# Recurrent block: the lower levels' products in four groups of 32 stationary columns, and a new order of a level's steps on VectorE

## The chip, the cores and the metric

One core of one Trainium2 chip runs the whole program. The metric is the device time of one execution in microseconds (us). The engines are named as in the profile: PE (TensorE's matmuls), PEld (its weight loads), DVE (VectorE), ACT (ScalarE), POOL (GpSimd), SP (SyncE, which here only issues DMAs).

## The reference

The program computes two transformer-like blocks in a row over 256 tokens with 1024 features, in fp32. The change touches only the HGRN2 mixer, the first mixer of the second block. It has 8 heads of 128 key features and 128 value features:

```
proj = h @ w_in                      # (256, 4096), split in q, fz, inp, og
q = silu(q);  f = lb + (1 - lb) * sigmoid(fz);  k = 1 - f;  logf = log(f)
# per head, with a state S of 128 x 128:
#   S_t = diag(f_t) S_{t-1} + (1 - f_t) inp_t^T ;   o_t = S_t^T q_t
cum    = cumsum(logf)
scores[t, s] = sum_n q[t,n] * k[s,n] * exp(cum[t,n] - cum[s,n])     for s <= t
o[t]   = sum_s scores[t, s] * inp[s]
y      = (rms_norm(o, out_norm) * sigmoid(og)) @ w_out
```

## The kernel before

**The streamed weights.** All weights come as 374 parts of 128x1024 fp32 through a ring of four buffers (`raw`). ACT rounds a part to a high half (`hi`, L315), DVE subtracts it from the part to get the low half (`lo`, L779), and PE multiplies high by high, high by low and low by high (L1541 to L1543, for token tiles L1663 to L1665). PE waits for `lo_ready` ahead of a tile; `multiplied` is a wait for `part_done`, by which PE tells that it has used a part. A call `step(name, j)` on DVE is `lo` for the part three behind part j of that phase. A tile goes to one of four PSUM banks (0 to 3), and PE may not begin tile n before tile n-4 is evicted (`free_bank`, on the semaphore `evacuated`).

**The recurrence as levels.** The 256 tokens are two halves of 128 (index z), the second in reversed order. In a half, the scores between tokens are made by levels. Level 0 is the diagonal, level 1 neighbours, and level l (2 to 7) takes blocks of 2^l tokens: keys of the early half of a block against queries of its later half, both decayed to the block's middle, so that no exponent is positive. Level 8 is between the two halves. One level needs, in this order:

- `level_args(l)` on DVE: two subtractions of 128x1024 (`args_later`, L1168, and `args_earlier`, L1172) write the exponents of queries and keys into the buffer `EB[l % 2]`. It waits on `lev_mm` until the matmuls of level l-2, which read the same buffer, are done. For level 8 it is one subtraction (L1179).
- `level_decay(l)` on ACT: exp over the buffer, 128x2048 (L624).
- `level_queries(l)` on DVE: the queries times their decay, 128x1024 (L1190), which raises `x_up`.
- `level_mm(l)` on PE (L1845): for each head one fp32 matmul with 128 stationary columns (all keys of the head) and 128 moving ones (64 queries of either half). `pair_mm` (L1832) makes levels 0 and 1 with 64 moving columns, one matmul for a head and half. Results go to banks 4 to 7, two banks for a level (g = 0, 1), `lev_mm` counts the banks. An fp32 matmul leaves two records in the trace.
- `take(l)` for levels 0 to 5 on DVE (L1205): two predicated copies of 128x512 from PSUM into the score matrix `PD`, under the mask `LM` (which pairs belong to the level). `take_wide(l)` for levels 6 and 7 on ACT (L638) copies rectangles. `lev_sel` counts both.

**The order around it.** The mixer's stage `hi` (the input part, 8 parts in four pairs, `hi_tile(n, tok)` for a pair n and a half) and `hg` (the gate, `hg_tile(t)`, 8 parts) run on PE between the levels: `hi_tile(0,0)`, `pair_mm(0)`, `hi_tile(0,1)`, `pair_mm(1)`, and then for l = 2 to 7 two tiles and `level_mm(l)`: `hi_tile(2,·)`, `hi_tile(4,·)`, `hi_tile(6,·)`, `hg_tile(0)` and `(1)`, `(2)` and `(3)`, `(4)` and `(5)`. Then `hg_tile(6)`, `across_mm` (level 8, L1855), `hg_tile(7)`, and the eight heads' outputs (`head`, L1893 to L1895), mixed with the first tiles of the output projection `ho`. PE, DVE and ACT each have their order written out by hand; SP loads a part as soon as its buffer is free. A `hi_tile(n,0)` needs the low halves of parts n and n+1, `hg_tile(t)` that of part t; `hg` follows `hi` in the stream, so part hg+t is part hi+8+t. On DVE the loop before is

```
for l in range(3, LEVELS + 1):
    level_args(l)
    if l - 2 < TAKEN: take(l - 2)
    n = 2 * (l - 2)
    step("hi", n)
    level_queries(l)
    if l >= 7: gate_evict(2 * (l - 7)), gate_evict(2 * (l - 7) + 1)
    step("hi", n + 1)
```

`gate_evict(t)` (L810) empties the bank of `hg_tile(t)`. ACT makes the high halves in `token_pair` and `gate_tile`, between its `level_decay`s.

Of the kernel before, what the change touches and what calls it, by code (L numbers as in the profile page):

```python
# [15 lines left out]
I32 = mybir.dt.int32  # L16
# [4 lines left out]
P = 128  # L21
S = 256
D = 1024
C = D // P
# [44 lines left out]
LEVELS, TAKEN = 8, 6  # L69

# [3 lines left out]
def build(nc, stream, par_d, x_d, wf_d, table_d, onehot_d, ident_d, mask_d, lmask_d, out_d):  # L74
    scr = nc.dram_tensor("bias_rows", [H_MOBA, P, EXT], F32, kind="Internal")
    row = nc.dram_tensor("bias_row", [H_MOBA, EXT], F32, kind="Internal")
    with ExitStack() as ctx:
# [57 lines left out]
        LM = flat(F[:, 48:51, :]).bitcast(I32).rearrange("p (l z j) -> p l z j", l=TAKEN, z=2)  # L135
# [11 lines left out]
        U_CUM, U_KK, U_CK, U_QS, U_PD, U_EB = 8, 16, 16, 24, 68, (0, 60)  # L147
# [23 lines left out]

        H_REV, RSTD_REV = u_two[:, 2 * C:3 * C, :, 0:P], F[:, 51, 0:P]
# [133 lines left out]
        def _(act):  # L306
# [319 lines left out]
            def take_wide(l):  # L626
# [3 lines left out]
                for g in range(2):  # L630
                    act.wait_ge(lev_sel, 2 * l + g)
                    act.wait_ge(lev_mm, 2 * l + g + 1)
# [6 lines left out]
                    last.then_inc(lev_sel, 1)  # L639

# [9 lines left out]
            for t in range(0, 4, 2):  # L650
                gate_tile(t)
                gate_tile(t + 1)
                level_decay(7 + t // 2)
            take_wide(6)
# [6 lines left out]
            for g in range(2):  # L661
                act.wait_ge(lev_mm, 2 * LEVELS + g + 1)
                A(PX[:, 4 * g:4 * g + 4, :], bank[4 + g][:, :].rearrange("p (h t) -> p h t", h=4),
                  ACT.Copy).then_inc(px_copied, 1)
# [104 lines left out]
        def _(dve):  # L769
# [405 lines left out]
            def level_args(l):  # L1175

                dve.wait_ge(lev_mm, 2 * (l - 1))
# [14 lines left out]
            def take(l):  # L1192
# [3 lines left out]
                n = P // b  # L1196
                for g in range(2):
                    if l >= 1:
                        dve.wait_ge(lev_sel, 2 * (l - 1) + g + 1)
                    dve.wait_ge(lev_mm, 2 * l + g + 1)  # L1200
                    half = early(U_PD, 1) if l == 0 else later(U_PD, l)
                    dst = half[:, :, 4 * g * n:4 * (g + 1) * n, :].rearrange("p z (c n) i -> p z c n i", c=4)
                    pick = LM[:, l:l + 1, :, :].rearrange("p l z (n i) -> p z l n i", i=h)
                    src = bank[4 + 2 * (l % 2) + g][:, :].rearrange("p (z c n i) -> p z c n i", z=2, c=4, i=h)
                    v.copy_predicated(dst, pick.to_broadcast([P, 2, 4, n, h]), src).then_inc(lev_sel, 1)  # L1205
# [11 lines left out]
            dve.wait_ge(pd_zero, 1)  # L1217
# [5 lines left out]
            level_queries(2)  # L1223
            step("hi", 1)
            for l in range(3, LEVELS + 1):
                level_args(l)
                if l - 2 < TAKEN:
                    take(l - 2)
                n = 2 * (l - 2)
                step("hi", n)  # L1230
                level_queries(l)
# [137 lines left out]
        def _(pool):  # L1369
# [70 lines left out]
            g.memset(PD, 0.0).then_inc(pd_zero, 1)  # L1440
            for pair in range(2):
# [83 lines left out]
        def _(pe):  # L1525
# [299 lines left out]
            def pair_mm(l):  # L1825

                keys, queries = (KK_T, early(U_QS, 1)) if l == 0 else (EB_T[1], later(U_QS, 1))
                for g in range(2):
                    for c in range(4 * g, 4 * g + 4):
                        for z in range(2):  # L1830
                            o = z * S + c % 4 * (P // 2)
                            last = mm(bank[4 + 2 * l + g][:, o:o + P // 2], keys[:, z, c, :],  # L1832
                                      queries[:, z, c * (P // 2):(c + 1) * (P // 2), 0], start=True, stop=True)
                    last.then_inc(lev_mm, 1)

            def level_mm(l):
# [3 lines left out]
                pe.wait_ge(x_up, l - 1)  # L1840
                for g in range(2):
                    pe.wait_ge(lev_sel, 2 * (l - 2) + g + 1)
                    out = bank[4 + 2 * (l % 2) + g][:, :].rearrange("p (z c j) -> p z c j", z=2, c=4)
                    for c in range(4 * g, 4 * g + 4):
                        last = mm(out[:, :, c % 4, :], keys[:, c, :], queries[:, :, c, :], start=True, stop=True)  # L1845
                    last.then_inc(lev_mm, 1)

            def across_mm():

                pe.wait_ge(x_up, LEVELS - 1)  # L1850
                for g in range(2):
                    pe.wait_ge(lev_sel, 2 * (LEVELS - 2) + g + 1)
# [48 lines left out]
            pe.wait_ge(lev_sel, 2 * LEVELS)  # L1901
# [176 lines left out]
```

## Time and profile before

| | us |
|---|---|
| median of three runs (1168.82 to 1169.49) | 1168.86 |
| the profiled execution, whole | 1168.89 |
| its span, first to last instruction | 1167.1 |
| PE busy in the span | 1149.9 |
| DVE busy | 877.7 |
| ACT busy | 697.2 |
| POOL busy | 380.7 |

The profile is of one execution. A group of rows below is either of the page (busy time and share of the span for each engine), of a timeline (start and length in us, engine, line of the kernel, output and inputs, and in brackets the idle time of the engine before it and what released it), of the waits (who waited for whom, us in total, times, longest), or of groups of instructions by line and shape (count, busy us, mean ns of one). "128*64 128x128" is a matmul over 128 rows with 64 stationary and 128 moving columns. Ends of matmuls are modelled, and two matmuls in a row overlap in their lengths, so a pace is read from start to start.

### The profile page before, as it was taken

The page shows a single profiled execution, that of the slowest core. Times are in us where ns is not written, and L with a number is a line of the kernel's source. Part 1 is how long each engine was busy: PE and PEld are TensorE (multiplying, and loading weights), DVE is VectorE, ACT ScalarE, POOL GpSimd, SP SyncE. Part 2 cuts the span into 40 slices and gives each one's busy share as a digit, 9 for nine tenths or more (in the row PEclk, how much of TensorE's full clock was granted, in tenths as well). Part 3 has the DMA queues.
Part 4 walks back from the last instruction along what each step waited for, and adds up shares of the span by engine and source line. Part 5 has one row for each costly group of instructions (what it writes and reads, how often), then busy time and mean ns, then how long its engine had stood idle before and what let it go on. Part 6 is the DMA issues. An engine that isn't in the chain of part 4 may idle for free.

```text
span 1167.1 us, 23692 instructions
## 1 busy us (share of the span) xinstructions
PE 1149.9 (99%) x8394; PEld 1083.1 (93%) x8394; DVE 877.7 (75%) x1360; ACT 697.2 (60%) x1133; POOL 380.7 (33%) x385
## 2 busy tenths in 40 slices
PE   9999999999999999999999999999999999999997
PEld 8999999999999999899999988888899998888886
DVE  6976897967688888448899687777765777777753
ACT  6588657645566566446747666665555556766553
POOL 3375000502246664222000245445320015554432
PEclk9999999999999999999999999999999999999999
DMA  7566444676355556663534356557756445655662
GB/s 260 157 190 215 139 127 127 193 239 218 124 159 182 180 180 195 205 195 109 180 102 143 104 180 196 193 183 238 227 167 202 147 123 165 204 188 182 208 204 74
DMA packets 56706, 204.32 MB, mean 175 GB/s; under 512 B 6832, under 2 KB 6984, under 8 KB 56512
## 3 DMA queue, kind: packets, MB, share of 16 engines
q1 hardware_dynamic: 54432, 197.35, 54.1%
q0 software_dynamic: 1632, 5.00, 1.2%
q8 instruction: 46, 0.75, 0.3%
q10 hardware_dynamic: 576, 1.05, 0.2%
q14 instruction: 20, 0.16, 0.0%
HBM read 202.29 MB, written 2.63 MB: 176 GB/s over the span
## 4 chain that ended last, share of the span: by engine, by line
PE 89%; DVE 6%; ACT 3%; issue 1%; DMA 0%; DVEq 0%; SPq 0%; ACTq 0%
PE bank L1535 21%; PE bank L1541 15%; PE bank L1542 14%; PE bank L1543 14%; PE bank L1536 12%; PE bank L1538 2%; DVE w_lo L779 2%; PE bank L1663 2%; PE bank L1664 2%; PE bank L1665 2%; ACT w_hi L315 1%; PE bank L1754 1%; PE bank L1845 1%; PE bank L1744 1%; PE bank L1634 1%
## 5 line engine op out<-in xcount | busy, mean ns | idle before, releaser
L779 DVE TENSOR_TENSOR w_lo<-raw,w_hi 128x1024 fp32r<-128x1024 f32 x374 | 468.6, 1256 | 133.3 <-ACT w_hi L315 131.7
L315 ACT ACTIVATE w_hi<-raw 128x1024 fp32r<-128x1024 f32 x374 | 391.6, 1053 | 139.0 <-PE bank L1543 77.6
L1541 PE MATMUL bank<-h_two,w_hi 128*128 128x256 f32 x1184 | 343.5, 290 | 4.2 <-DVE w_lo L779 3.9
L1542 PE MATMUL bank<-h_two,w_hi 128*128 128x256 f32 x1184 | 334.8, 283 | 0.0
L1543 PE MATMUL bank<-h_two,w_lo 128*128 128x256 f32 x1184 | 334.8, 283 | 0.0
L1541 PEld LDWEIGHTS bank<-h_two,w_hi 128*128 128x128 f32 x1184 | 226.8, 192 | 8.6 <-issue 5.1
L1542 PEld LDWEIGHTS bank<-h_two,w_hi 128*128 128x128 f32 x1184 | 226.9, 192 | 0.8
L1543 PEld LDWEIGHTS bank<-h_two,w_lo 128*128 128x128 f32 x1184 | 226.8, 192 | 0.0
L1535 PE MATMUL bank<-h_two,w_hi 128*128 128x512 f32 x616 | 221.6, 399 | 1.1 <-DVE h_two L804 0.9
L1536 PE MATMUL bank<-h_two,w_lo 128*128 128x256 f32 x704 | 183.6, 281 | 0.0
L1535 PE MATMUL bank<-u_two,w_hi 128*128 128x512 f32 x455 | 161.2, 397 | 0.0
L1536 PEld LDWEIGHTS bank<-h_two,w_lo 128*128 128x128 f32 x704 | 132.9, 189 | 7.9
L1535 PEld LDWEIGHTS bank<-h_two,w_hi 128*128 128x128 f32 x616 | 115.9, 188 | 26.2 <-DVE h_two L804 1.3
L1536 PE MATMUL bank<-u_two,w_lo 128*128 128x256 f32 x476 | 130.2, 281 | 0.0
L1463 POOL TENSOR_TENSOR work<-work 128x256 f32<-128x256 f32 x66 | 66.6, 1010 | 174.9 <-DVE work L1311 115.5
L1541 PE MATMUL bank<-u_two,w_hi 128*128 128x256 f32 x392 | 111.9, 285 | 0.4 <-DVE u_two L1252 0.4
L1543 PE MATMUL bank<-u_two,w_lo 128*128 128x256 f32 x392 | 110.9, 283 | 0.0
L1542 PE MATMUL bank<-u_two,w_hi 128*128 128x256 f32 x392 | 110.9, 283 | 0.0
L1468 POOL TENSOR_TENSOR u_two<-work,u_two 128x256 f32 x66 | 101.4, 1537 | 12.1 <-POOL u_two L1466 12.1
L1535 PEld LDWEIGHTS bank<-u_two,w_hi 128*128 128x128 f32 x455 | 85.4, 188 | 19.9
L324 ACT ACTIVATE work<-bank 128x256 f32<-128x256 f32 x109 | 41.5, 380 | 94.4 <-PE bank L1538 94.4
L1536 PEld LDWEIGHTS bank<-u_two,w_lo 128*128 128x128 f32 x476 | 89.9, 189 | 2.0
(255 smaller groups left out, 1763.6 us busy)
## 6 DMA issues: line engine op xcount, KB each, us to landing
raw<-in_stream SPq DMA_DIRECT2D x374, 512.0 KB, 3.5
bias_rows<-bias_row POOLq DMA_DIRECT2D x1, 1536.0 KB, 15.1
work<-in_x_t SPq DMA_DIRECT2D x2, 512.0 KB, 5.6
work<-in_x_t POOLq DMA_DIRECT2D x1, 1024.0 KB, 6.1
work<-bias_rows POOLq DMA_DIRECT2D x1, 1024.0 KB, 10.8
out<-work ACTq DMA_DIRECT2D x4, 256.0 KB, 2.5
work<-bias_rows POOLq DMA_DIRECT2D x1, 512.0 KB, 5.8
work<-in_lmask POOLq DMA_DIRECT2D x1, 384.0 KB, 6.8
```

The source lines that it names most:

```text
L315: A(w_hi[:, slot, :], raw[:, slot, :], ACT.Copy).then_inc(hi_ready, 1)
L324: A(LOW[:, t % BANKS, :], bank[t % BANKS][:, S:2 * S], ACT.Copy).then_inc(low_out, 1)
L779: v.tensor_tensor(w_lo[:, slot, :], raw[:, slot, :], w_hi[:, slot, :].bitcast(F32), ALU.subtract).then_inc(lo_ready, 1)
L1463: g.tensor_tensor(PB[:, pair, :], GB[:, pair, :], YB[:, 2 * pair + 1, :], ALU.mult).then_inc(pair_free, 1)
L1468: g.tensor_tensor(dst_l, PB[:, pair:pair + 1, :], dst_h.bitcast(F32), ALU.subtract).then_inc(ul_ready, 1)
L1535: mm(pair, w_hi[:, slot, s], both, start=start, stop=False)
L1536: last = mm(own, w_lo[:, slot, s], r_two[:, 0, :], start=False, stop=False)
L1538: last = mm(pair, w_hi[:, slot, s], both, start=False, stop=True)
L1541: mm(out, w_hi[:, slot, s], r_two[:, 0, :], start=start, stop=False)
L1542: mm(out, w_hi[:, slot, s], r_two[:, 1, :], start=False, stop=False)
L1543: return mm(out, w_lo[:, slot, s], r_two[:, 0, :], start=False, stop=stop)
L1663: mm(out, x_hi, w_hi[:, s0:s0 + 2, f], start=(b == 0), stop=False)
```

## The change

- In `pair_mm` and `level_mm` a head's keys are cut into four groups q of 32 columns. Group q is the stationary operand of its own matmul, its result goes to PSUM partitions 32q to 32q+31, and it meets only queries of the same 32 tokens (levels 0 to 5: 16 or 2x16 moving columns; level 6: 32; level 7: 64). `pair_mm` has 64 matmuls for 16, `level_mm` 32 for 8.
- Levels 0 to 5 so have 256 columns in all (8 heads x 32) and fit into half a bank; each of them has one bank, `bank[4 + l % 4]`, and raises `lev_mm` once. `lev_before(l)` gives the count before level l.
- `take(l)` is one predicated copy of 128x256 elements, into a compact matrix `PDC`; the mask is a quarter as wide. Behind `level_decay(7)` ACT copies `PDC` out to `PD` in four copies of 32x512 (`spread`), for which the heads wait (`pd_spread`). POOL clears `PDC` too.
- On DVE the loop is turned: a pass l issues the queries of level l, then the arguments of level l+1, the take of level l-1, and then the steps.

```diff
@@ -169,6 +172,18 @@
             h = 2 ** (l - 1)
             return units(u, C * P, [[C * P // 2, 2], [h, C * P // (2 * h)], [1, h]])
 
+        def compact(l):
+
+            if l == 0:
+                return units(U_PDC, 0, [[C * GRP + 1, 2], [2, C * GRP // 2], [1, 1]])
+            h = 2 ** (l - 1)
+            return units(U_PDC, h, [[C * GRP - h, 2], [2 * h, C * GRP // (2 * h)], [1, h]])
+
+        def lev_before(l):
+
+            return l if l <= TAKEN else TAKEN + 2 * (l - TAKEN)
+
+        pd_spread = sem("pd_spread")
         H_REV, RSTD_REV = u_two[:, 2 * C:3 * C, :, 0:P], F[:, 51, 0:P]
         h_turned, rstd_turned = sem("h_turned"), sem("rstd_turned")
         FG_T, CUM_T, KK_T, CK_T, QS_T, PD_T = (toks(x) for x in (FG, CUM, KK, CK, QS, PD))
@@ -628,8 +643,8 @@
                 b = 2 ** l
                 h = b // 2
                 for g in range(2):
-                    act.wait_ge(lev_sel, 2 * l + g)
-                    act.wait_ge(lev_mm, 2 * l + g + 1)
+                    act.wait_ge(lev_sel, lev_before(l) + g)
+                    act.wait_ge(lev_mm, lev_before(l) + g + 1)
                     src = bank[4 + 2 * (l % 2) + g][:, :].rearrange("p (z c j) -> p z c j", z=2, c=4)
                     for z in range(2):
                         for n in range(P // b):
@@ -637,6 +652,14 @@
                             cols = slice(n * b + (1 - z) * h, n * b + (1 - z) * h + h)
                             last = A(PD_T[rows, z, 4 * g:4 * g + 4, cols], src[rows, z, :, n * h:(n + 1) * h], ACT.Copy)
                     last.then_inc(lev_sel, 1)
+
+            def spread():
+
+                act.wait_ge(lev_sel, TAKEN)
+                for q in range(P // GRP):
+                    rows = slice(q * GRP, q * GRP + GRP)
+                    last = A(PD_T[rows, :, :, rows], PDC_T[rows, :, :, :], ACT.Copy)
+                last.then_inc(pd_spread, 1)
 
             def gate_tile(t):
                 multiplied(PART["hg"] + t)
@@ -651,6 +674,8 @@
                 gate_tile(t)
                 gate_tile(t + 1)
                 level_decay(7 + t // 2)
+                if t == 0:
+                    spread()
             take_wide(6)
             gate_tile(4)
             gate_tile(5)
@@ -1174,7 +1199,7 @@
 
             def level_args(l):
 
-                dve.wait_ge(lev_mm, 2 * (l - 1))
+                dve.wait_ge(lev_mm, lev_before(l - 1))
                 if l == LEVELS:
                     v.tensor_tensor(EB_T[0][:, 0, :, :], CUM_T[:, 0, :, P - 1:P].to_broadcast([P, C, P]),
                                     CK_T[:, 0, :, :], ALU.subtract).then_inc(arg_ready, 1)
@@ -1193,16 +1218,14 @@
 
                 b = 2 ** max(l, 1)
                 h = b // 2
-                n = P // b
-                for g in range(2):
-                    if l >= 1:
-                        dve.wait_ge(lev_sel, 2 * (l - 1) + g + 1)
-                    dve.wait_ge(lev_mm, 2 * l + g + 1)
-                    half = early(U_PD, 1) if l == 0 else later(U_PD, l)
-                    dst = half[:, :, 4 * g * n:4 * (g + 1) * n, :].rearrange("p z (c n) i -> p z c n i", c=4)
-                    pick = LM[:, l:l + 1, :, :].rearrange("p l z (n i) -> p z l n i", i=h)
-                    src = bank[4 + 2 * (l % 2) + g][:, :].rearrange("p (z c n i) -> p z c n i", z=2, c=4, i=h)
-                    v.copy_predicated(dst, pick.to_broadcast([P, 2, 4, n, h]), src).then_inc(lev_sel, 1)
+                n = GRP // b
+                if l >= 1:
+                    dve.wait_ge(lev_sel, l)
+                dve.wait_ge(lev_mm, l + 1)
+                dst = compact(l).rearrange("p z (c n) i -> p z c n i", c=C)
+                pick = LM[:, l:l + 1, :, :].rearrange("p l z (n i) -> p z l n i", i=h)
+                src = bank[4 + l % 4][:, 0:S].rearrange("p (z c n i) -> p z c n i", z=2, c=C, i=h)
+                v.copy_predicated(dst, pick.to_broadcast([P, 2, C, n, h]), src).then_inc(lev_sel, 1)
 
             def gate_evict(t):
                 multiplied(PART["hg"] + t)
@@ -1214,21 +1237,21 @@
             args_later(2)
             step("hi", 0)
             dve.wait_ge(lm_in, 16)
-            dve.wait_ge(pd_zero, 1)
+            dve.wait_ge(pd_zero, 2)
             take(0)
             dve.wait_ge(logk_ready, 1)
             v.tensor_tensor(CK, CUM, LK, ALU.subtract).then_inc(ck_ready, 1)
             dve.wait_ge(ck_ready, 1)
             args_earlier(2)
-            level_queries(2)
-            step("hi", 1)
-            for l in range(3, LEVELS + 1):
-                level_args(l)
-                if l - 2 < TAKEN:
-                    take(l - 2)
+            for l in range(2, LEVELS + 1):
+                level_queries(l)
+                if l < LEVELS:
+                    level_args(l + 1)
+                if l - 1 < TAKEN:
+                    take(l - 1)
                 n = 2 * (l - 2)
-                step("hi", n)
-                level_queries(l)
+                if l >= 3:
+                    step("hi", n)
                 if l >= 7:
                     dve.wait_ge(evacuated, TILE["hg"])
                     gate_evict(2 * (l - 7))
@@ -1438,6 +1461,7 @@
             pool.dma_start(LM, lmask_d).then_inc(lm_in, 16)
             pool.wait_ge(ml, C)
             g.memset(PD, 0.0).then_inc(pd_zero, 1)
+            g.memset(PDC, 0.0).then_inc(pd_zero, 1)
             for pair in range(2):
                 g.memset(PB[:, pair, 0:1], 0.0).then_inc(pair_free, 1)
 
@@ -1825,31 +1849,46 @@
             def pair_mm(l):
 
                 keys, queries = (KK_T, early(U_QS, 1)) if l == 0 else (EB_T[1], later(U_QS, 1))
-                for g in range(2):
-                    for c in range(4 * g, 4 * g + 4):
-                        for z in range(2):
-                            o = z * S + c % 4 * (P // 2)
-                            last = mm(bank[4 + 2 * l + g][:, o:o + P // 2], keys[:, z, c, :],
-                                      queries[:, z, c * (P // 2):(c + 1) * (P // 2), 0], start=True, stop=True)
-                    last.then_inc(lev_mm, 1)
+                for c in range(C):
+                    for z in range(2):
+                        for q in range(P // GRP):
+                            o, rows = z * P + c * GRP // 2, slice(q * GRP, q * GRP + GRP)
+                            n = (c * P + q * GRP) // 2
+                            last = mm(bank[4 + l][rows, o:o + GRP // 2], keys[:, z, c, rows],
+                                      queries[:, z, n:n + GRP // 2, 0], start=True, stop=True)
+                last.then_inc(lev_mm, 1)
 
             def level_mm(l):
 
                 keys = EB_T[l % 2][:, 0, :, :]
                 queries = EB_T[l % 2][:, 1, :, :].rearrange("p c t -> p (c t)").rearrange("p (z c j) -> p z c j", z=2, c=C)
                 pe.wait_ge(x_up, l - 1)
+                if l < TAKEN:
+                    if l >= 4:
+                        pe.wait_ge(lev_sel, l - 3)
+                    out = bank[4 + l % 4][:, 0:S].rearrange("p (z c j) -> p z c j", z=2, c=C)
+                    for c in range(C):
+                        for q in range(P // GRP):
+                            rows, js = slice(q * GRP, q * GRP + GRP), slice(q * GRP // 2, (q + 1) * GRP // 2)
+                            last = mm(out[rows, :, c, :], keys[:, c, rows], queries[:, :, c, js], start=True, stop=True)
+                    last.then_inc(lev_mm, 1)
+                    return
                 for g in range(2):
-                    pe.wait_ge(lev_sel, 2 * (l - 2) + g + 1)
+                    pe.wait_ge(lev_sel, 5 + g if l == 6 else 4)
                     out = bank[4 + 2 * (l % 2) + g][:, :].rearrange("p (z c j) -> p z c j", z=2, c=4)
                     for c in range(4 * g, 4 * g + 4):
-                        last = mm(out[:, :, c % 4, :], keys[:, c, :], queries[:, :, c, :], start=True, stop=True)
+                        for q in range(P // GRP):
+                            rows = slice(q * GRP, q * GRP + GRP)
+                            z, js = (q // 2, slice(0, P // 2)) if l == 7 else (q % 2, slice(q // 2 * GRP, q // 2 * GRP + GRP))
+                            last = mm(out[rows, z, c % 4, js], keys[:, c, rows], queries[:, z, c, js], start=True,
+                                      stop=True)
                     last.then_inc(lev_mm, 1)
 
             def across_mm():
 
                 pe.wait_ge(x_up, LEVELS - 1)
                 for g in range(2):
-                    pe.wait_ge(lev_sel, 2 * (LEVELS - 2) + g + 1)
+                    pe.wait_ge(lev_sel, lev_before(LEVELS - 2) + g + 1)
                     for j in range(4):
                         c = 4 * g + j
                         last = mm(bank[4 + g][:, j * P:(j + 1) * P], EB_T[0][:, 0, c, :], EB_T[0][:, 1, c, ::-1],
@@ -1898,7 +1937,8 @@
                 for t in range(3):
                     tile(0, PART["ho"] + t, TILE["ho"] + t, u_two, oh_lo, 0, range(b, b + 1))
 
-            pe.wait_ge(lev_sel, 2 * LEVELS)
+            pe.wait_ge(lev_sel, lev_before(LEVELS))
+            pe.wait_ge(pd_spread, 1)
             pe.wait_ge(px_copied, 2)
             for c in range(C):
                 head(c)
@@ -2059,7 +2099,8 @@
         b = 2 ** max(l, 1)
         h = b // 2
         for z in range(2):
-            q = np.array([n * b + i + (h if (l > 0) != (z == 1) else 0) for n in range(P // b) for i in range(h)])[None, :]
+            q = np.array([n * b + i + (h if (l > 0) != (z == 1) else 0) for n in range(GRP // b) for i in range(h)])[None, :]
+            q = q + s // GRP * GRP
             same = s // b == q // b
             later_keys.append(s == q if l == 0 else same if l == 1 else same & ((s // h) % 2 == z))
     lmask = np.stack(later_keys, axis=1).astype(np.int32)
```

## Rows read from the trace of the kernel before

**Rows 1.** The page: engines' busy us, share, instructions; the chain by engine.

```profile
PE 1149.9 (99%) x8394; PEld 1083.1 (93%) x8394; DVE 877.7 (75%) x1360; ACT 697.2 (60%) x1133; POOL 380.7 (33%) x385
...
PE 89%; DVE 6%; ACT 3%; issue 1%; DMA 0%; DVEq 0%; SPq 0%; ACTq 0%
```

**Rows 2.** Waits, 576 to 652: waiting line, releaser, us in total, times, longest.

```profile
PE bank L1663 <- DVE w_lo L779: 1.9, 3, 1.4
```

**Rows 3.** PE timeline: start, length, line, operation, [idle before, releaser].

```profile
580.87 3.73 PE L1832 MATMUL bank<-work 128*128 128x64 f32 x32
...
596.70 1.95 PE L1845 MATMUL bank<-work 128*128 128x128 f32 x16
...
600.04 0.39 PE L1663 MATMUL bank<-w_hi,h_two 128*128 128x256 f32 x1 [1.39 <-DVE w_lo L779]
...
608.03 0.39 PE L1663 MATMUL bank<-w_hi,h_two 128*128 128x256 f32 x1 [0.18 <-DVE w_lo L779]
...
613.88 1.95 PE L1845 MATMUL bank<-work 128*128 128x128 f32 x16
...
615.59 0.36 PE L1541 MATMUL bank<-h_two,w_hi 128*128 128x256 f32 x1
```

**Rows 4.** DVE timeline of the same stretch.

```profile
584.65 1.32 DVE L1205 COPY_PREDICATED work<-work,bank 128x512 f32<-128x512 int32 x1 [0.39 <-PE bank L1832]
...
598.73 1.25 DVE L779 TENSOR_TENSOR w_lo<-raw,w_hi 128x1024 fp32r<-128x1024 f32 x1
...
602.16 1.23 DVE L1168 TENSOR_TENSOR work<-work 128x1024 f32<-128x1024 f32 x1
...
604.43 2.50 DVE L1205 COPY_PREDICATED work<-work,bank 128x512 f32<-128x512 int32 x2
...
619.57 1.33 DVE L1205 COPY_PREDICATED work<-work,bank 128x512 f32<-128x512 int32 x2
...
629.98 0.75 DVE L810 TENSOR_TENSOR work<-bank,work 128x256 f32<-128x256 f32 x2
```

**Rows 5.** Groups by shape: xcount, busy us, mean ns of one.

```profile
L1845 PE MATMUL bank<-work 128*128 128x128 f32 x96 | 11.7, 275 | 0.0
...
L1845 PEld LDWEIGHTS bank<-work 128*128 128x128 f32 x96 | 11.2, 192 | 0.0
...
L1776 PEld LDWEIGHTS bank<-att_pt,work 128*64 128x64 f32 x96 | 5.1, 136 | 2.3 <-issue 2.2
```

**Rows 6.** PE and PEld timelines around twelve records with 64 stationary columns.

```profile
138.92 0.60 PE L1754 MATMUL bank<-work 128*128 128x256 f32 x2
139.45 0.88 PE L1776 MATMUL bank<-att_pt,work 128*64 128x128 f32 x12
140.26 0.39 PE L1541 MATMUL bank<-h_two,w_hi 128*128 128x256 f32 x1
...
139.45 0.64 PEld L1776 LDWEIGHTS bank<-att_pt,work 128*64 128x64 f32 x12 [0.33 <-issue]
```

**Rows 7.** An ACT copy; a window: busy of PE, PEld, DVE, ACT.

```profile
649.55 0.62 ACT L676 ACTIVATE work<-work 128x512 f32<-128x512 f32 x1
...
596.00:646.00 50.00, 48.43 (x410) 48.04 (x409) 44.53 (x47) 33.60 (x42) 0.00 (x0) 1.00 0.45 147
```

**Rows 8.** PE timeline at 336 and the end; a later window (clock: 0.50).

```profile
336.21 0.38 PE L1541 MATMUL bank<-h_two,w_hi 128*128 128x256 f32 x1 [2.03 <-DVE w_lo L779]
336.43 0.28 PE L1542 MATMUL bank<-h_two,w_hi 128*128 128x256 f32 x1
336.54 0.28 PE L1543 MATMUL bank<-h_two,w_lo 128*128 128x256 f32 x1
...
1159.02 0.70 PE L1574 MATMUL bank<-work,ones 128*128 128x256 f32 x2 [0.61 <-ACT work L756]
...
1162.00:1163.00 1.00, 0.00 (x0) 0.00 (x0) 1.00 (x2) 0.00 (x0) 0.58 (x1) 0.50 0.07 27
```

**Rows 9.** PE timeline of the kernel's start.

```profile
1.13 7.28 PE L1584 MATMUL bank<-ones 128*128 128x128 f32 x48 [1.13 <-DVE ones L842]
```

More of the change, by code:

```diff
@@ L69 @@
 LEVELS, TAKEN = 8, 6
+GRP = 32
 UNITS = 82
@@ L134, in build @@
         INP, OG = F[:, 32:40, :], F[:, 40:48, :]
-        LM = flat(F[:, 48:51, :]).bitcast(I32).rearrange("p (l z j) -> p l z j", l=TAKEN, z=2)
+        LM = flat(F[:, 48:49, :])[:, 0:TAKEN * GRP].bitcast(I32).rearrange("p (l z j) -> p l z j", l=TAKEN, z=2)
+        PDC = F[:, 49:51, :]
         EB = [F[:, 0:8, :], F[:, 60:68, :]]
@@ L145, in toks @@
             return flat(ap).rearrange("p (z c t) -> p z c t", z=2, c=C)
-        U_CUM, U_KK, U_CK, U_QS, U_PD, U_EB = 8, 16, 16, 24, 68, (0, 60)
+        PDC_T = flat(PDC).rearrange("p (z c t) -> p z c t", z=2, c=C)
+        U_CUM, U_KK, U_CK, U_QS, U_PDC, U_EB = 8, 16, 16, 24, 49, (0, 60)
         def units(u, start, dims):
@@ L661, in _ @@
             for g in range(2):
-                act.wait_ge(lev_mm, 2 * LEVELS + g + 1)
+                act.wait_ge(lev_mm, lev_before(LEVELS) + g + 1)
                 A(PX[:, 4 * g:4 * g + 4, :], bank[4 + g][:, :].rearrange("p (h t) -> p h t", h=4),
```

## The prediction

> **What bounds the kernel now.** I read the page's busy and chain parts first: PE is busy for 99% of the span and carries 89% of the chain that ended last [rows 1]. So whatever adds PE time, or stops PE, in the stretch from 577 to 646 us lengthens the kernel one for one; nothing behind it has PE idle time to give back. Next the waits of that stretch [rows 2]: PE stood idle 1.9 us in three places, each time for a low half of the weights from L779 on DVE. DVE is the only engine that PE waits for here. The PE timeline [rows 3] shows where: the first token tile after a level's matmuls came 1.39 us late at 600.04 and 0.18 us late at 608.03, and at 615.59 it followed without idle time. Without a wait the next matmul starts 0.24 us before the modelled end of a level's records (613.88+1.95 against 615.59), so the two cost 1.39+0.24 = 1.63 us and 0.18+0.24 = 0.42 us, 2.05 us together. The DVE timeline [rows 4] names the releaser: the L779 of 598.73, which is `step("hi", 2)`, ended at 599.98, and the tile began at 600.04 [rows 3, 4]. What matters most is its place: it ran before `level_args(4)` (L1168 and L1172, from 602.16 to 604.43), whose wait for level 2's matmuls had by then long been met.
>
> **Part 1, the matmuls.** Before, two `pair_mm` with 16 calls and six `level_mm` with 8 leave 64 and 96 records, two for a call [rows 5]. Records follow each other at (1.95-0.275)/15 = 0.112 us with 128 moving columns and at (3.73-0.273)/31 = 0.112 us with 64 [rows 3]: the 128 stationary columns set the pace, not the moving ones. 160 x 0.112 = 17.9 us. After, two times 64 calls and six times 32 are 320 calls, 640 records, with 32 stationary columns and 16 to 64 moving ones. The nearest row is L1776 with 64 stationary columns in two column groups: (0.88-0.27)/11 = 0.055 us [rows 6]. Its loads take 136 ns, those of 128 columns 192 [rows 5]: 56/64 = 0.875 ns for a column, so a load of 32 occupies 28 ns. I take 0.029: 18.6 us, **+0.7**. Upper bound: nothing goes faster than L1776, 0.055, 35.2 us, +17.3. Lower bound: L1776 streams 128 columns of fp32 in 0.055, where 256 columns take 0.60-0.38 = 0.22 a record [rows 6], that is 0.11 for 128; two column groups overlapped. If four overlap their loads too, 28/4 = 7 ns, 4.5 us, -13.4. I keep to 0.029 because L1776 stands exactly at half the pace of 128 columns, as a serial load would have it.
>
> The Trainium skill (TensorE: Matmul & The Clock Gate, "Part 3: Packing small matmuls — row/col tiling") gives packed tiles about 4 ns each beyond the first; by that 640 records would be an estimated 2.6 us, 15.3 less than now, and the rule speaks for this change. The same page's "Wait — 56ns, not 53.3ns?" says that starts never come closer than about 25 ns; by that it would be an estimated 16.0 us, 1.9 less. The 0.055 of L1776 lies above both and excludes neither [rows 6].
>
> **Part 2, the change of tile shape.** After twelve L1776 records the next wide matmul starts at 140.26, 0.81 after 139.45, where 12 x 0.055 = 0.66: 0.15 lost. Before them L1754 at 138.92 with 2 x 0.22 ends its turn at 139.36, and L1776 starts at 139.45: 0.09. Eight blocks x 0.24 = **+1.9**. Below: zero, as around L1845; above: the 0.33 that stands before PEld's first load of that group, 8 x 0.33 = 2.6 [rows 6].
>
> **Part 3, the order on DVE: this decides.** Each pass of the new loop issues `level_queries(l)`, `level_args(l+1)`, `take(l-1)` and only then `step("hi", 2(l-2))`. `level_args(l+1)` overwrites the buffer that level l-1 uses and waits for its matmuls. On PE the tile right behind `level_mm(l-1)` needs the very step that then is queued behind this wait. Pass 3: `level_args(4)` waits for the end of `level_mm(2)`; `hi_tile(4,0)`, next on PE, needs `lo_ready` of part hi+5, which is `step("hi",2)`. From PE's last record to its next: 0.05 until DVE starts (584.60 to 584.65), two argument tensors at 1.13 [rows 4], the take, the L779 with 1.25, 0.06 to PE. A take is one instruction of 256 elements in place of two of 512: levels 0 to 2 took 1.25 to 1.32 each and levels 3 to 5 0.67 (2.50 and 1.33 for two), so 0.62 and 0.33 [rows 4]. To the idle time the same 0.24 is added.
> - `hi_tile(4,0)`: 0.05+2.26+0.62+1.25+0.06+0.24 = 4.5 us.
> - `hi_tile(6,0)` behind `level_mm(3)`, with take(3): 4.2 us.
> - `hg_tile(1)` behind `level_mm(4)`: the same 4.2, of which `hg_tile(0)` covers 24 x 0.12 = 2.9 (its part was made a pass earlier): 1.3 us. `hg_tile(3)` behind `level_mm(5)`: 1.3 us.
> - `hg_tile(4)` behind `level_mm(6)` needs the bank of `hg_tile(0)`, so `gate_evict(0)` (L810). Before, that ran at 629.98, ahead of `level_args(8)` [rows 4]. After, it stands behind `level_args(8)`, which waits for `level_mm(6)`: 0.05+1.13+1.13+0.42+0.06+0.24 = 3.0 us.
>
> Sum 14.3, less the old 2.05: **+12.2 us**. I walked the other queues with the same durations: ACT's exponentials (1.91) end before DVE comes to their queries, the queries end before the level's matmuls, and the high halves on ACT come before their low halves, so no second wait adds to these. Bounds: 10.6 if the takes are free (1.6 less); 17.1 if they keep their old lengths.
>
> **Part 4, covered edits.** The spread is four ACT copies of 32x512, about 0.6 each by L676 [rows 7], 2.4 us behind `level_decay(7)`; it delays the high halves of hg+6 and hg+7, needed more than 8 us later, and ACT was idle for 16 of the 50 us from 596 [rows 7]. Were that cover gone, it would cost its 2.4 us. The takes fall from some 11.6 us (2 x 1.32, 2 x 2.50, 3 x 1.33) to 2.9 [rows 4], which gives DVE 8.7 us back, but DVE then only waits longer in `level_args`; after `hi_tile(4,0)` none of it reaches PE. The second memset on POOL and the smaller mask load are issued right behind the merge, some 300 us before their first use, where POOL waits. At the heads, `px_copied` and `pd_spread` are ready before `hg_tile(7)` ends: zero.
>
> **Part 5, the clock.** PE will stand still for some 4.2 us twice. The trace has one stop of 2.03 us (at 336.21) after which records went on 0.11 apart (336.43 to 336.54), and the end of the kernel, where the granted clock was at 0.50, the lower of the two levels (1.2 GHz), by 1162.00, 2.3 us after the last matmul's end at 1159.72 [rows 8]. A restart at the lower level is seen at the start: 48 records in 7.28-0.27 = 7.0 us, where 47 x 0.112 = 5.3: 1.75 lost [rows 9]. I take two falls, **+3.5**. Bounds: none, 0; three falls (the 2.8 us stop at `hg_tile(4)` too) of twice the price, 10.5.
>
> **The sum.** +0.7 +1.9 +12.2 +3.5 = +18.3 on the profiled execution's own 1168.89 (span 1167.1 and 1.8 around it), 0.03 from the median of the runs, 1168.86: **1187.2 us**.
>
> **The rivals.**
> - **B, a pace of 0.055 for the small matmuls** (two instructions a record, and no row that shows them come faster): for it, no record in the trace lies closer; against it, the load durations fall with the columns. 1168.9+17.3+1.9+12.2+3.5 = 1203.8.
> - **C, the clock holds**: for it, the stop of 2.03 us at 336; against it, the end. 1183.7.
> - **D, four column groups side by side**, the mechanism that ends not slower: the levels shrink to 4.5 us (-13.4) with no cost for the shape and a clock that holds: -13.4+12.2 = -1.2, 1167.7. It decides from a pace of (17.9-12.2)/640 = 9 ns down. For it: the overlap in L1776; against it: 0.055 is six times that. It is the case of the rule of packed tiles named above.
> - **E, the stops of PE don't come**, because I misjudge what the tile behind a level waits for. Then +0.7+1.9-2.05 = +0.6, 1169.4, no change. Against it: the releases by L779 are just this wait [rows 2].
>
> **Chances.** Forecast 0.57, B 0.17, C 0.18, D 0.04, E 0.04. What this kernel's measurement can tell from no change is about 0.2%, 2.3 us: D is split between faster and same, E is same. Slower 0.93, same 0.05, faster 0.02. The range leaves out D, E and the upper edge of B: 1177 to 1203.
>
> **What would show it.** PE idle before L1663 behind DVE's low half: two of 4 us, at `hi_tile(4,0)` and `hi_tile(6,0)`; two of 1.1 before wide matmuls of hg, one of 2.8 behind L810; DVE idle before the argument tensors, released by the level matmuls; six predicated copies of 0.3 to 0.6; 384 + 256 small records 0.029 apart; records twice as far apart for some 3 us after each long stop. If the idle times before L1663 are as before, part 3 is wrong; if the levels' records stand over 0.04 apart, part 1 is.

## The result and the profile after

The changed kernel takes 1179.12 us (median of four runs, 1176.94 to 1179.4) against 1168.84 us: ratio 1.008, 95% interval 1.0068 to 1.0093. It is slower by 10.3 us, in the forecast range and the forecast direction; 1187.2 was named. The profiled execution is the shortest of the four: 1176.94, span 1175.1, so 8.0 above the one before, of which 1.0 had passed before the stretch of the change began.

The page and the waits from 576 to 665 (waiting line, releaser, us in total, times, longest), to be read beside [rows 1, 2]. L1687 is now the first matmul of a token tile, L1565 of a feature tile, L804 the low half, L835 the eviction, L1193 and L1197 the two argument tensors, L1873 `level_mm` for levels 2 to 5 and L1883 for 6 and 7.

```profile
PE 1145.3 (97%) x8874; PEld 1077.2 (92%) x8874; DVE 869.1 (74%) x1354; ACT 700.1 (60%) x1137; POOL 376.1 (32%) x386
```

```profile
DVE work L1193 <- PE bank L1873: 13.5, 3, 6.0
...
PE bank L1687 <- DVE w_lo L804: 11.0, 3, 6.7
...
PE bank L1565 <- DVE work L835: 2.9, 1, 2.9
...
PE bank L1565 <- DVE w_lo L804: 1.7, 2, 0.9
```

PE is busy 4.6 us less (1145.3 for 1149.9 [rows 1]) and yet the kernel is longer: PE waits 11.0 us for low halves before token tiles, where it waited 1.9, and DVE waits 13.5 us for level matmuls before its arguments, where it had not waited at all. The two wait for each other. A stop is below a time in which PE stands idle ahead of a matmul; a wide matmul is one of the `hi` or `hg` tiles, with 128 stationary and 256 moving columns. The PE timeline shows the places (start, length, operation, idle time before and its releaser), beside [rows 3]:

```profile
581.98 1.27 PE L1857 MATMUL bank<-work 128*32 128x16 f32 x128
583.17 0.39 PE L1687 MATMUL bank<-w_hi,u_two 128*128 128x256 f32 x1
...
593.39 0.76 PE L1873 MATMUL bank<-work 128*32 128x32 f32 x64
...
600.85 0.58 PE L1687 MATMUL bank<-w_hi,h_two 128*128 128x256 f32 x1 [6.70 <-DVE w_lo L804]
...
608.10 0.76 PE L1873 MATMUL bank<-work 128*32 128x32 f32 x64
...
612.78 0.39 PE L1687 MATMUL bank<-w_hi,h_two 128*128 128x256 f32 x1 [3.92 <-DVE w_lo L804]
...
620.21 0.76 PE L1873 MATMUL bank<-work 128*32 128x32 f32 x64
620.90 0.39 PE L1565 MATMUL bank<-h_two,w_hi 128*128 128x256 f32 x1
...
624.89 0.38 PE L1565 MATMUL bank<-h_two,w_hi 128*128 128x256 f32 x1 [0.85 <-DVE w_lo L804]
...
632.63 0.39 PE L1565 MATMUL bank<-h_two,w_hi 128*128 128x256 f32 x1 [0.84 <-DVE w_lo L804]
...
639.37 0.36 PE L1565 MATMUL bank<-h_two,w_hi 128*128 128x256 f32 x1 [2.91 <-DVE work L835]
```

The 128 records of `pair_mm` start (1.27-0.183)/127 = 0.0086 us apart (a record is 0.183 long), the 64 of a level (0.76-0.196)/63 = 0.009. From its first record to the next wide matmul a `pair_mm` costs 1.19 us (was 3.54), a level 0.69 (was 1.71), level 7 1.03. And the five stops stand where they were forecast: `hi_tile(4,0)`, `hi_tile(6,0)`, `hg_tile(1)`, `hg_tile(3)`, `hg_tile(4)`. DVE's side of the first two, beside [rows 4]:

```profile
594.07 1.26 DVE L804 TENSOR_TENSOR w_lo<-raw,w_hi 128x1024 fp32r<-128x1024 f32 x1
595.61 1.22 DVE L1215 TENSOR_TENSOR work<-work 128x1024 f32<-128x1024 f32 x1 [0.28 <-ACT work L639]
596.75 1.22 DVE L1193 TENSOR_TENSOR work<-work 128x1024 f32<-128x1024 f32 x1
597.89 1.22 DVE L1197 TENSOR_TENSOR work<-work 128x1024 f32<-128x1024 f32 x1
599.02 0.72 DVE L1228 COPY_PREDICATED work<-work,bank 128x256 f32<-128x256 int32 x1
599.53 2.39 DVE L804 TENSOR_TENSOR w_lo<-raw,w_hi 128x1024 fp32r<-128x1024 f32 x2
...
608.90 1.23 DVE L1193 TENSOR_TENSOR work<-work 128x1024 f32<-128x1024 f32 x1 [5.84 <-PE bank L1873]
610.04 1.22 DVE L1197 TENSOR_TENSOR work<-work 128x1024 f32<-128x1024 f32 x1
611.18 0.43 DVE L1228 COPY_PREDICATED work<-work,bank 128x256 f32<-128x256 int32 x1
611.51 2.35 DVE L804 TENSOR_TENSOR w_lo<-raw,w_hi 128x1024 fp32r<-128x1024 f32 x2
```

At 608.90 DVE had stood idle for 5.84 us until the level's matmuls (608.10) ended, and then did arguments, take and low half while PE stood. At the first stop it is another matter: DVE did not wait at 596.75; it was late by itself, since PE had come there over 3 us earlier. The windows (busy of PE, PEld, DVE, ACT, POOL; then granted clock, DMA share, GB/s) show what the stops did to the clock: from 597.0 to 603.8 it was at 0.50, the 1.2 GHz level, and matmuls of 256 columns stood 0.213 apart in place of 0.12. Behind the second stop, which ended at 612.78, it fell only at 614.1, with PE at work, and rose at 617.4.

```profile
594.00:596.00 2.00, 0.15 (x18) 0.04 (x4) 1.72 (x3) 2.00 (x3) 0.00 (x0) 1.00 0.00 0
596.00:598.00 2.00, 0.00 (x0) 0.00 (x0) 2.00 (x3) 2.00 (x3) 0.00 (x0) 0.75 0.66 219
598.00:600.00 2.00, 0.00 (x0) 0.00 (x0) 2.00 (x3) 1.06 (x2) 0.00 (x0) 0.50 0.11 43
...
602.00:604.00 2.00, 2.00 (x12) 2.00 (x11) 1.06 (x1) 0.00 (x0) 0.00 (x0) 0.55 0.86 260
```

**The account.** From the first `hi` tile to the first head the stretch was 67.93 us before and is 75.05 after, +7.1; behind it both kernels need the same (521.28 and 521.14). A block's time is taken from its first record to the next wide matmul, a stop's beyond that:

| | us |
|---|---|
| level blocks, start to start: 17.3 before (7.04 and 6 x 1.71), 6.9 after (2.39, 5 x 0.70, 1.03) | -10.4 |
| the old stops | -2.05 |
| the new stops: 6.8, 4.0, 1.1, 1.1, 3.0 | +15.9 |
| two spells at the lower clock: `hi(4,·)` 7.25 and `hi(6,·)` 7.43 us in place of 5.86 | +3.0 |
| the other six tiles, each about 0.1 longer: their last record ahead of a block of small matmuls takes 0.21 in place of 0.12 | +0.6 |
| sum | +7.1 |

### The profile page after: what moved, and what is told of

The parts are those of the page before. It is cut to its first block, busy times and chain, and to the rows that moved or that the text cites. A ratio compares the mean times of both kernels' runs of the same rounds, so it can differ in the third digit from the quotient of the medians.

```text
span 1175.1 us, 24644 instructions
## 1 busy us (share of the span) xinstructions
PE 1145.3 (97%) x8874; PEld 1077.2 (92%) x8874; DVE 869.1 (74%) x1354; ACT 700.1 (60%) x1137; POOL 376.1 (32%) x386
## 4 chain that ended last, share of the span: by engine, by line
PE 88%; DVE 7%; ACT 3%; issue 1%; DMA 0%; DVEq 0%; SPq 0%; ACTq 0%
PE bank L1559 21%; PE bank L1565 15%; PE bank L1566 14%; PE bank L1567 14%; PE bank L1560 12%; PE bank L1562 2%; DVE w_lo L804 2%; PE bank L1687 2%; PE bank L1688 2%; PE bank L1689 2%; ACT w_hi L330 1%; PE bank L1778 1%; DVE work L1197 1%; PE bank L1768 1%; PE bank L1658 1%
## 5 line engine op out<-in xcount | busy, mean ns | idle before, releaser
L804 DVE TENSOR_TENSOR w_lo<-raw,w_hi 128x1024 fp32r<-128x1024 f32 x374 | 470.0, 1260 | 131.7 <-ACT w_hi L330 130.1
L1565 PE MATMUL bank<-h_two,w_hi 128*128 128x256 f32 x1184 | 344.3, 291 | 7.7 <-DVE w_lo L804 4.4
L1565 PEld LDWEIGHTS bank<-h_two,w_hi 128*128 128x128 f32 x1184 | 227.5, 192 | 12.5 <-DVE w_lo L804 6.0
L1565 PE MATMUL bank<-u_two,w_hi 128*128 128x256 f32 x392 | 111.9, 285 | 0.4 <-DVE u_two L1275 0.4
L1492 POOL TENSOR_TENSOR u_two<-work,u_two 128x256 f32 x66 | 98.0, 1486 | 12.1 <-POOL u_two L1490 12.1
```

The costliest lines, as they stand in the source:

```text
L804: v.tensor_tensor(w_lo[:, slot, :], raw[:, slot, :], w_hi[:, slot, :].bitcast(F32), ALU.subtract).then_inc(lo_ready, 1)
L1492: g.tensor_tensor(dst_l, PB[:, pair:pair + 1, :], dst_h.bitcast(F32), ALU.subtract).then_inc(ul_ready, 1)
L1565: mm(out, w_hi[:, slot, s], r_two[:, 0, :], start=start, stop=False)
```

## Experiments

The kernel before ran beside each group of them, at 1169.7, 1169.8 and 1169.5 us; ratios are to it. Differences to the changed kernel, which ran beside 1168.84, are up to 1 us off if taken from the medians and not from the ratios. The diffs here are shortened: bodies of an `if` are drawn onto its line, `n` stands for `2 * (l - 2)`, and the wait for `evacuated` ahead of the two `gate_evict` is left out.

**old_order** is the changed kernel with DVE's old order.

```diff
-            for l in range(2, LEVELS + 1):
-                level_queries(l)
-                if l < LEVELS: level_args(l + 1)
-                if l - 1 < TAKEN: take(l - 1)
-                if l >= 3: step("hi", 2 * (l - 2))
+            level_queries(2)
+            step("hi", 1)
+            for l in range(3, LEVELS + 1):
+                level_args(l)
+                if l - 2 < TAKEN: take(l - 2)
+                step("hi", 2 * (l - 2))
+                level_queries(l)
```

> The changed kernel, with DVE's loop as it was before: arguments of level l, take, step, queries, step. Theory 1 (the order on DVE costs the time, the small matmuls gain it): the stops of PE at hi_tile(6,0), hg_tile(1), hg_tile(3) and hg_tile(4) go, the one at hi_tile(4,0) shrinks from 6.7 to about 3.4 us because PE comes there earlier than DVE can follow; with levels of 6.9 in place of 17.3 us this gives about 1161 us, 8 below the kernel before, and the clock holds. Theory 2 (the groups of 32 columns and the takes cause the slowdown): 1177 to 1180, as the changed kernel.

Measured: 1168.69 us (1166.14 to 1170.21), ratio 0.999 (0.9982 to 0.9999). Direction right, size missed: 10.4 us below the changed kernel, but not 1161. The stop at `hi_tile(4,0)` was 2.9 for the expected 3.4. The one at `hg_tile(4)`, which was expected to go, was 2.19, for its eviction, and two more came: 0.94 at `hg_tile(6)` and 1.26 at the first head. And the clock (third last column of these windows), which was expected to hold, fell at 597.4, behind the 2.9 us stop, which had ended at 596.04:

```profile
597.00:598.00 1.00, 1.00 (x9) 1.00 (x8) 0.55 (x2) 1.00 (x2) 0.00 (x0) 0.69 0.74 164
598.00:599.00 1.00, 1.00 (x6) 1.00 (x6) 1.00 (x1) 0.87 (x1) 0.00 (x0) 0.50 0.86 348
```

That profile is of the run of 1166.32 us. The runs mostly go with their mean clock: 1166.3 at 0.997, 1168.6 at 0.994, 1170.1 at 0.993, but one of 1167.3 is at 0.993 too. What the runs above it lost, and where, no trace shows.

**steps_first** keeps the new place of the queries and moves two things ahead of the wait.

```diff
                 level_queries(l)
+                if l >= 3: step("hi", n)
+                if l >= 7: gate_evict(2 * (l - 7)), gate_evict(2 * (l - 7) + 1)
                 if l < LEVELS: level_args(l + 1)
                 if l - 1 < TAKEN: take(l - 1)
-                if l >= 3: step("hi", n)
-                if l >= 7: gate_evict(2 * (l - 7)), gate_evict(2 * (l - 7) + 1)
                 step("hi", n + 1)
```

> The changed kernel, its queries still ahead of the next arguments, but step('hi', n) and the two gate evictions put ahead of level_args(l+1). Theory 1: what costs is only that the step and the eviction stand behind a wait for a level's matmuls, so this is as fast as the old order, about 1161 us, with one stop of some 4 us at hi_tile(4,0). Theory 3 (queries ahead of arguments is itself the cost, by late exponentials): stops of 1 us or more before level matmuls, 1165 or more.

Measured: 1164.55 us (1164.01 to 1165.38), 0.996 (0.9947 to 0.9973). 14.6 below the changed kernel by these few lines, and no stop before a level's matmuls: the queries' place is not the cost. Left are a stop of 3.22 at `hi_tile(4,0)`, for the expected 4, 0.56 at `hg_tile(4)`, and the lower clock from 599.3 to 602.7, which made the two tiles there 7.44 us long for 5.95. The clock and the small stop are 2.1 of the 3.5 us above 1161; the rest is not traced.

**order_only** puts the new loop into the kernel before, with its own matmuls and takes.

> The kernel before, with only DVE's loop in the new order. Theory 1: level matmuls and takes of the old size, and the stops come: 6.4 at hi_tile(4,0), 5.2 at hi_tile(6,0), 2.3 each at hg_tile(1) and hg_tile(3), 3.0 at hg_tile(4), 19.2 less the old 2.05, and two falls of the clock, 3.5: about 1189 us. Theory 2 (the groups cause the slowdown): 1169, no change.

Measured: 1191.86 us (1188.73 to 1194.17), 1.0183 (1.0169 to 1.0196). The stops, forecast at 6.4, 5.2, 2.3, 2.3 and 3.0:

```profile
605.01 0.58 PE L1663 MATMUL bank<-w_hi,h_two 128*128 128x256 f32 x1 [6.55 <-DVE w_lo L779]
...
618.88 0.58 PE L1663 MATMUL bank<-w_hi,h_two 128*128 128x256 f32 x1 [4.79 <-DVE w_lo L779]
...
634.14 0.39 PE L1541 MATMUL bank<-h_two,w_hi 128*128 128x256 f32 x1 [1.92 <-DVE w_lo L779]
...
645.38 0.50 PE L1541 MATMUL bank<-h_two,w_hi 128*128 128x256 f32 x1 [1.94 <-DVE w_lo L779]
```

The fifth was 2.88. The order alone costs 22 us; the changed kernel is some 12 faster than that through its matmuls and takes. In this profile the clock fell in or behind each of the five stops, not only at two, and the kernel's runs reach from 1188.7 (near the expected 1189) at a mean clock of 0.994 to 1194.2 at 0.988.

**q_outer**: old_order with the group loop outermost; the same matmuls in another order. The diff shows `pair_mm`; `level_mm` has the same turn.

```diff
-                    for c in range(C):
-                        for q in range(P // GRP):
+                    for q in range(P // GRP):
+                        for c in range(C):
```

> old_order with the loop over the four column groups outside the loop over heads, so that matmuls in a row share a group; the same matmuls. If the pace of 9 ns a record comes from four groups working side by side, records now stand 28 ns or more apart, the levels take about 18.6 us, part of which falls into the stop at hi_tile(4,0): 1168 to 1171 us. If short matmuls are fast by themselves, 9 ns stays and the time is that of old_order, about 1161.

Measured: 1170.29 us (1170.03 to 1171.84), 1.0008 (0.9999 to 1.0017).

```profile
581.97 3.93 PE L1857 MATMUL bank<-work 128*32 128x16 f32 x128
...
598.69 1.91 PE L1873 MATMUL bank<-work 128*32 128x32 f32 x64
```

(3.93-0.183)/127 = 0.0295 us a record, in place of 0.0086, and (1.91-0.197)/63 = 0.0272 for a level. So the pace that I had forecast for the change is that of small matmuls which share a column group with their neighbours; the change's own loop gives neighbours different groups, and then records of the same length start three times as close. Against old_order it is only 1.6 us more: the longer blocks fill DVE's lateness, no stop is left at a tile of this stretch, and the granted clock is 1.00 from 577 to 650.

**evict_first**: the changed kernel, the two `gate_evict` moved behind `level_queries(l)`, nothing else.

> The changed kernel with only the two gate evictions put ahead of level_args(8); the steps stay behind. Theory 1: the stop of 2.9 us at hg_tile(4) goes, the other four stay: 1176 us. Rival (an eviction earlier only moves the stop to the next tile or to the low half): 1178 to 1179.

Measured: 1175.02 us (1174.37 to 1176.36), 1.0049 (1.0035 to 1.0063): 4.1 below the changed kernel (3.6 by the ratios). The stop at `hg_tile(4)` is gone and nothing takes its place; the other four stay (6.70, 3.92, 0.86, 0.86). What is beyond the stop's 2.9 would fit a fall of the clock at it in most of the changed kernel's runs; such a fall is seen in clock_kept, in the changed kernel itself it is not shown.

**clock_kept** fills the two long stops with matmuls.

```diff
                 level_mm(l)
+                if l in (2, 3):
+                    for _ in range(24 if l == 2 else 14):
+                        mm(bank[4][:, S:S + P], ones[:, :], ones[:, :], start=True, stop=True)
```

> The changed kernel with matmuls of ones into an unused half of bank 4 behind level_mm(2) (24 calls, 5.4 us) and level_mm(3) (14 calls, 3.1 us), inside PE's two long stops; nothing else. If the lower clock after the stops costs its 2.8 us (14 and 16 records 0.213 apart in place of 0.119), the granted clock stays 1.00 and the median is about 1176.3, and the runs lie closer together than 1176.9 to 1179.4. If it costs nothing, 1179.

Measured: 1175.63 us (1174.9 to 1175.95), 1.0049 (1.0036 to 1.0063), 3.5 below. PE's idle time at the two places fell to 0.50 and 0.60 us, DVE did the same work at the same moments, and the clock stayed at 1.00 there: the two tiles of `hi(4,·)` took 5.93 us for 7.25, those of `hi(6,·)` 5.95 for 7.43, 2.8 less. It fell instead in the stop of 2.91 at `hg_tile(4)`, from 635.2 to 642.0, and `hg_tile(4)` and `(5)` took 8.59 for 5.92, 2.7 more. Between the two profiled runs the stretch is therefore nearly equal, 74.95 and 75.05; the 3.5 us are between the medians, and the changed kernel's profiled run is its fastest, 2.2 below its median.

**takes_x4**: steps_first with DVE's saving given back.

```diff
+                for k in range(3):
+                    spare = flat(att_pt)[:, k * S:(k + 1) * S].rearrange(...)
+                    v.copy_predicated(spare, pick.to_broadcast([P, 2, C, n, h]), src)
                 v.copy_predicated(dst, pick.to_broadcast([P, 2, C, n, h]), src).then_inc(lev_sel, 1)
```

> steps_first with each take followed by three more copies of its size into spare memory: DVE gets back 3 x 2.9 = 8.7 us, about what the compact takes saved; the copies' results are not used. If DVE's room counts (6.1 us of its work against 6.5 of PE's a level), PE stops again before level tiles and the time is 3 to 6 us above steps_first, 1168 to 1171. If the compact takes were worth nothing and only the matmuls gain, 1164.5 to 1165.

Measured: 1167.09 us (1166.0 to 1167.61), 0.9978 (0.9969 to 0.9987): 2.5 above steps_first, a little less than expected. The 18 spare copies took DVE 6.6 us, not the 8.7 that were reckoned; the change had saved 8.1 (takes of 3.5 us in all for 11.6). The stop at `hi_tile(4,0)` grew from 3.22 to 5.05, that at `hg_tile(4)` from 0.56 to 1.68.

**ahead** is the version that the first four pointed to.

```diff
+            level_args(3)
+            level_queries(2)
+            step("hi", 1)
+            step("hi", 2)
+            take(1)
+            for l in range(3, LEVELS + 1):
+                level_queries(l)
+                if 4 <= l < 7: take(l - 2)
+                if l >= 7: gate_evict(2 * (l - 7)), gate_evict(2 * (l - 7) + 1)
+                if l < LEVELS: level_args(l + 1)
+                if l == 6: take(l - 1)
+                step("hi", 2 * (l - 2) + 1)
+                if l < LEVELS: step("hi", 2 * (l - 2) + 2)
```

> The changed kernel with DVE's steps put so that PE should not stop: level_args(3) in DVE's idle time before the queries of level 2, steps 1 and 2 right behind those, and from there each pass queries(l), take(l-2), evictions, args(l+1), and the steps of the coming pass. Theory 1 (the gain of the small matmuls, 10.4 us, stands in full once no step waits behind a level's matmuls, and without a stop of about 3 us the clock holds): no stop over 1 us at the level blocks, clock 1.00 from 577 to 645, 10.4 + 2.05 below the kernel before, about 1157 to 1159 us. Rival (DVE's total of work in the stretch bounds it, so that each stop taken away comes back in front of the next level's matmuls): 1163 to 1165, as steps_first.

Measured: 1158.39 us (1157.76 to 1159.28), 0.9907 (0.9892 to 0.9922), the fastest kernel here: 11.4 us below the kernel before and 20.7 below the change. The level blocks follow each other without a stop of PE, and the tile behind each starts 0.7 to 0.8 us after its first record, 1.03 behind level 7; the clock is 1.00 from 577 to 645:

```profile
592.54 0.76 PE L1879 MATMUL bank<-work 128*32 128x32 f32 x64
599.24 0.76 PE L1879 MATMUL bank<-work 128*32 128x32 f32 x64
...
605.88 0.76 PE L1879 MATMUL bank<-work 128*32 128x32 f32 x64
612.51 0.76 PE L1879 MATMUL bank<-work 128*32 128x32 f32 x64
...
619.14 0.76 PE L1889 MATMUL bank<-work 128*32 128x32 f32 x64
```

From the first tile to the first head it needs 56.80 us, 11.1 less than before; 10.4 + 2.05, less some 0.8 for the records ahead of the eight small blocks, were in reach.

**ahead_wide**, the same order on the kernel before.

> The kernel before (128 stationary columns, two takes a level) with DVE's order of the run ahead. If that order is good by itself, it takes away the 2.05 us that PE lost after the levels 2 and 3: about 1167.7, against 1169.8 of the kernel before. If DVE, which here has 8.7 us more in takes, has no room for it, stops come back before later tiles: 1169.5 or more. Either way 10 us above ahead: the small matmuls' part.

Measured: 1168.3 us (1167.24 to 1168.49), 0.9985 (0.9976 to 0.9994), a gain of 1.2: the stops after levels 2 and 3 go, one of 0.66 appears at `hg_tile(4)`. So some 10 of the 11.4 us of ahead need the small matmuls and takes.

**ahead_q_outer**, ahead with the group loop outermost.

> The run ahead with the loop over the four column groups outermost, so that matmuls in a row share a group. In q_outer part of the cost fell into a stop at hi_tile(4,0); here PE never stops, so the whole difference between 0.029 and 0.009 us a record should stand: levels of about 17.8 us in place of 6.9, 1158.4 + 10.9 = 1169.3 us. If the order of groups did nothing by itself, 1158.4.

Measured: 1169.97 us (1169.12 to 1171.77), 1.0003 (0.9994 to 1.0012), 11.6 above ahead. Here too the clock is 1.00 from 577 to 650. With no stop to fall into, the order of the groups is worth as much as the whole gain.

**ahead_takes_x4**, ahead with the spare copies of takes_x4.

> The run ahead with three more copies behind each take, into spare memory, results unused: 8.7 us more on DVE. By DVE's room (0.4 us a level) PE should stop again, 2 to 5 us in all: 1160.5 to 1163.5. If DVE's takes are covered in this order, 1158.4 to 1159.

Measured: 1165.45 us (1164.36 to 1166.12), 0.996 (0.9946 to 0.9974), 7.1 above ahead and more than the expected 2 to 5: stops of 0.94, 0.54, 0.62 and 3.35 us, and in the last the clock fell, from 624.3 to 631.1. The spare copies took 6.6 us here too. The compact takes are not free time; they are what leaves DVE its room beside a PE that has become faster.

## Why the prediction held, point by point

- **The order on DVE (part 3)** was right in the place of all five stops, with no sixth, and in the mechanism of four. Forecast 4.5, 4.2, 1.3, 1.3, 3.0; measured 6.8, 4.0, 1.1, 1.1, 3.0. order_only and steps_first show the cause from both sides. At the first DVE was to wait for `level_mm(2)`, and it didn't (no idle time before 596.75): I placed PE's arrival with level matmuls 0.029 us apart; with those of 0.009 PE came over 3 us earlier and met a DVE that had not even reached its wait. The step stands behind the arguments and the take all the same, but 3.22 us of this stop stay when it is put ahead of them (steps_first). Net of the old stops 13.8 for 12.2.
- **The small matmuls (part 1)** were the step that failed: +0.7 forecast, -10.4 measured. My sign of being wrong looked only for records over 0.04 us apart. I let the 32 columns' loads follow one another, 0.029 us a record. L1776 had shown two groups overlapping in their multiplies, and I did not carry that to their loads; the real pace, 0.0086, is near the lower bound of 0.007 and a third of what I took. q_outer gives 0.0295 where neighbours share a group, and that is the pace I took. The kernel is slower only because the stops and the clock outweigh this gain.
- **The rules of the Trainium skill** (TensorE: Matmul & The Clock Gate): the floor of about 25 ns between starts ("Wait — 56ns, not 53.3ns?") doesn't hold here, since records stand 8.6 ns apart; about 4 ns for a packed tile ("Part 3: Packing small matmuls — row/col tiling") is nearer, at half of what is measured.
- **The change of shape (part 2)** was about the right size. Ahead of a small block the last wide record takes 0.21 in place of 0.12, the 0.09 that I had read off L1776. What is lost behind a block is inside the -10.4: 1.19 us against 128 x 0.0086 = 1.10, 0.69 against 64 x 0.009 = 0.58. Reckoned as the forecast was, records times pace in part 1 and both ends here, part 1 is -11.9 (6.0 for 17.9) and part 2 +2.4 for 1.9, 0.6 of it because the blocks before took 17.3 and not 17.9.
- **The clock (part 5)**: two falls, 3.0 us for 3.5 in the profiled run; clock_kept takes both away, and the same tiles are 2.8 shorter. The price of a fall, 1.75, was read off [rows 9], but the granted clock of that stretch, 1 to 9 us, is recorded as 1.00, so that row shows slow records and no lower level; that the sum came near is partly luck, since other falls in these runs cost 1.3 to 2.7. The other three runs of the changed kernel, 2.0 to 2.5 us above the profiled one, have a mean clock of 0.989 to 0.991 against 0.992. That their difference is a third fall at `hg_tile(4)` is likely, not shown, as they have no trace.
- **Covered edits (part 4)**: the spread took 2.53 us and nobody waited for it. But the smaller takes (3.5 us in all, for the forecast 2.9) are not worthless on DVE: that holds only while DVE waits in `level_args` anyway.
- **The rivals**: B and E are refuted. D had the mechanism and nearly the pace, and its chance of 0.04 was too low; at its break-even of 9 ns the kernel is nevertheless 10 us slower, because D counted the stops at 12.2 and the clock and the change of shape at nothing. C, the clock that holds, is refuted by the windows.
- **The total** is 8.1 below the forecast: in the terms of the account -11.1 from part 1, -1.3 from part 2, +1.6 from the stops, -0.5 from the clock, +1.0 that the profiled run had lost before the stretch, and +2.2 by which the median lies above that run. The last two are in no term of the forecast, and without them the time would have been 1175.9, under the range's 1177. So the direction was right for its reason, the stops, while the range held by luck, with an error in part 1 as large as the whole change.

## What to carry over

When an edit moves a wait forward on an engine, list what stands behind it in that queue and who needs it next: here a low half and an eviction behind a wait for PE turned a gain of 11 us into a loss of 10. A faster consumer exposes its producer, so an order that was in balance must be planned again with the new durations; done so, the same matmuls gave 11.4 us.

## What the runs showed of the hardware

- Fp32 matmuls with 32 stationary columns in four column groups leave a record every 8.6 ns (16 moving columns) to 9.0 ns (2 x 16) when neighbours are in different groups, loads included, and every 29.5 and 27.2 ns when neighbours share one (q_outer). With 64 moving columns, neighbours in different groups, it was (1.10-0.218)/63 = 14 ns.
- The granted clock fell to its lower level in or behind each stop of 3.2 us and more, and in or behind some of 1.9 to 2.9; in old_order it fell 1.3 us and in steps_first 1.5 us after the stop had ended, while PE was at work again. It held behind the stop of 2.03 us of [rows 8], and behind the 2.91 in the changed kernel's profile. A fall cost 1.4 and 1.6 us in the changed kernel, and up to 2.7 elsewhere (clock_kept, and the second stop of order_only: 8.53 us for two tiles of 5.86). Runs of one kernel with different mean clocks differ by up to 4 us in old_order and 5.4 in order_only.
